# Second block of a two-block transformer kernel: gate projections moved between the query, key and value projections, head pairs every fourth chunk

## What is computed

```
h = rms_norm(x); proj = h @ w_in            # q, k, v, gate for three branches of 8 heads x 64,
                                            # q_idx (8 x 64), k_idx (64), w_idx (8), f_logit (8), merge_logit (3 x 1024)
oa = causal_attention(rope(qa), rope(ka), va) * silu(ga)
ob = causal_attention(rope(qb), rope(kb), vb, keys = top 64 of sum_h w_idx relu(rope(q_idx) . rope(k_idx))) * silu(gb)
oc = causal_attention(qc, kc, vc, logits += cumsum(log_sigmoid(f_logit + f_bias))) * silu(gc)
x  = x + (sum_n sigmoid(merge_n) * (o_n @ w_branch_n)) @ w_out
```

## Time and profile before

| | |
|---|---|
| runs of the kernel before | 1173.54 us median of 3 (1168.63 to 1174.01) |
| profiled execution | 1165.46 us, span 1163.5 us |
| PE, weight loads, DVE, ACT busy | 94%, 83%, 63%, 54% of the span |
| second block, first layer | from about 490 us to about 818 us |
| second block, second layer | from about 825 us to the end |
| mean granted PE clock | 0.975 |

### The profile page before, as it was taken

One profiled execution on the slowest core, in us unless ns is written; L12 is line 12 of the kernel. 1 busy time (PEld: TensorE's weight loads), 2 busy tenths in 40 slices (PEclk: granted clock), 3 DMA queues, 4 the chain that ended last, 5 costly groups with the idle time before them and its releaser, 6 DMA issues.

```text
span 1163.5 us, 20592 instructions
## 1 busy us (share of the span) xinstructions
PE 1090.6 (94%) x7991; PEld 966.3 (83%) x7991; DVE 736.1 (63%) x1559; ACT 627.8 (54%) x1279; POOL 2.6 (0%) x10
## 2 busy tenths in 40 slices
PE   5889999988977999989899999999998999999997
PEld 3667777766866778988899899999987998999997
DVE  4433466657465565889746776557788556766664
ACT  3344234565337654646677764445455767754443
POOL 0000000000000000000000000000000000000000
PEclk9999999998989999989999999999999999999998
DMA  9986471111313312535454566666444544566652
GB/s 317 291 260 203 150 217 52 42 55 54 100 55 90 90 57 85 157 93 143 128 145 128 141 168 181 183 185 185 119 119 118 146 127 132 160 182 183 183 178 73
DMA packets 264872, 165.04 MB, mean 142 GB/s; under 512 B 7092, under 2 KB 262824, under 8 KB 264776
## 3 DMA queue, kind: packets, MB, share of 16 engines
q1 hardware_dynamic: 264384, 163.02, 49.1%
q0 software_dynamic: 192, 0.66, 0.2%
q10 hardware_dynamic: 200, 0.06, 0.0%
HBM read 162.66 MB, written 1.05 MB: 141 GB/s over the span
## 4 chain that ended last, share of the span: by engine, by line
PE 75%; DVE 13%; ACT 6%; issue 4%; SPq 1%; DMA 1%; DVEq 0%; ACTq 0%
PE pj L1805 20%; PE pj L1806 20%; PE pj L1807 19%; DVE w_lo L1196 2%; PE tr L2250 1%; PE ac L2087 1%; PE sc L2075 1%; PE tr L1986 1%; PE sc L1979 1%; PE ac L2193 1%; ACT w_hi L743 1%; PE pj L1892 1%; DVE terms L1297 1%; PE ac L2000 1%; PE sc L2175 1%
## 5 line engine op out<-in xcount | busy, mean ns | idle before, releaser
L1805 PE MATMUL pj<-h_hi,w_hi 128*128 128x256 f32 (+1 forms) x1472 | 459.6, 312 | 14.6 <-DVE w_lo L1196 6.3
L1806 PE MATMUL pj<-h_lo,w_hi 128*128 128x256 f32 (+1 forms) x1472 | 446.7, 303 | 0.0
L1807 PE MATMUL pj<-h_hi,w_lo 128*128 128x256 f32 (+1 forms) x1472 | 446.7, 303 | 0.0
L1196 DVE TENSOR_TENSOR w_lo<-raw,w_hi 128x1024 fp32r<-128x1024 f32 (+1 forms) x258 | 309.7, 1202 | 187.9 <-ACT w_hi L743 186.9
L1805 PEld LDWEIGHTS pj<-h_hi,w_hi 128*128 128x128 f32 x1472 | 285.7, 194 | 42.9 <-issue 21.5
L743 ACT ACTIVATE w_hi<-raw 128x1024 fp32r<-128x1024 f32 (+1 forms) x258 | 267.4, 1038 | 53.9 <-PE pj L1807 53.9
L1806 PEld LDWEIGHTS pj<-h_lo,w_hi 128*128 128x128 f32 x1472 | 285.9, 194 | 10.3 <-issue 1.5
L1807 PEld LDWEIGHTS pj<-h_hi,w_lo 128*128 128x128 f32 x1472 | 285.3, 194 | 10.4
L1805 PE MATMUL pj<-m_hi,w_hi 128*128 128x256 f32 (+1 forms) x352 | 110.0, 312 | 10.1 <-DVE w_lo L1196 6.0
L1806 PE MATMUL pj<-m_lo,w_hi 128*128 128x256 f32 (+1 forms) x352 | 108.7, 309 | 0.0
L1807 PE MATMUL pj<-m_hi,w_lo 128*128 128x256 f32 (+1 forms) x352 | 108.5, 308 | 0.0
(11 more groups left out here) (308 smaller groups left out, 1319.7 us busy)
## 6 DMA issues: line engine op xcount, KB each, us to landing
raw<-in_w_in_dram SPq DMA_DIRECT2D x152, 512.0 KB, 3.8
ada_raw<-in_ada_w_dram SPq DMA_DIRECT2D x48, 512.0 KB, 6.9
raw<-in_even_w_in_dram SPq DMA_DIRECT2D x28, 512.0 KB, 4.8
raw<-in_w_branch_dram SPq DMA_DIRECT2D x24, 512.0 KB, 3.4
raw<-in_w_out_dram SPq DMA_DIRECT2D x16, 512.0 KB, 4.1
raw<-in_odd_w_in_dram SPq DMA_DIRECT2D x11, 512.0 KB, 4.1
raw<-in_even_w_out_dram SPq DMA_DIRECT2D x8, 512.0 KB, 3.7
raw<-in_odd_w_out_dram SPq DMA_DIRECT2D x8, 512.0 KB, 3.7
```

The source lines that it names most:

```text
L1196: last = nc.vector.tensor_tensor(lo, src, hi.bitcast(F32), ALU.subtract)
L1805: nc.tensor.matmul(dst, lh, rh, start=first, stop=False)
L1806: nc.tensor.matmul(dst, lh, rl, start=False, stop=False)
L1807: return nc.tensor.matmul(dst, ll, rh, start=False, stop=final)
```

## The change

Two gate chunks follow each two head pairs, from the second group on; the last two stand behind the first six `merge` chunks. Pairs move from slots 11 + 3t to 9 + 4t. The index scores move from slots 5, 7, 9, 10 to 11, 15, 19, 23, each between two pairs, the rotations of `qi_h` from slots 3, 4 to 7, 15, the rounds of the selection from slots 12 to 19 to 25 to 32, the small columns from 3 to 6, and the cumulative sum from 8 to 10. On DVE, in a pair's slot, `split_lo` and both reciprocals come straight behind `head_scores`; in other slots `split_lo` comes straight behind the evacuation. On ACT `split_hi` comes ahead of the small columns. Waits are added where `tanh` and `sc` are now shared in another order. No arithmetic and no load is added or removed; the loads come in the new order of chunks.

```diff
--- before.py
+++ after.py
@@ block2_chunks
-    out += [("g", t) for t in range(NTRIP)]
+        if t:
+            out += [("g", t - 2), ("g", t - 1)]
     for mp in range(4):
         out += [("merge", (b, 2 * mp + e)) for b in range(3) for e in range(2)]
+        if mp == 0:
+            out += [("g", NTRIP - 2), ("g", NTRIP - 1)]
         out += [("branch", (b, mp)) for b in range(3)]
@@ slots
-IDX_SLOT = {5: 0, 7: 1, 9: 2, 10: 3}
-PAIR_SLOT = {11 + 3 * t: t for t in range(NTRIP)}
-TOPK_SLOT = 12
-DECAY_SLOT = 8
-FEW_SLOT = 3
+PAIR_SLOT = {9 + 4 * t: t for t in range(NTRIP)}
+IDX_SLOT = {11 + 4 * m: m for m in range(4)}
+QI_SLOT = {7: 0, 15: 1}
+TOPK_SLOT = 25
+DECAY_SLOT = 10
+FEW_SLOT = 6
@@
+ROPE_ORDER = sorted([(2, "ki")] + [(s, ("qi", i)) for s, i in QI_SLOT.items()]
+                    + [(s + 1, c) for s, c in enumerate(B2_CHUNKS) if c[0] == "k" and BRANCH_ORDER[c[1] // 4] != FORGET])
+ROPE_ORDER = [name for _, name in ROPE_ORDER]
+
 def rope_number(pair):
-    return 3 + sum(BRANCH_ORDER[p // 4] != FORGET for p in range(pair))
+    return ROPE_ORDER.index(("k", pair))
+
+def rope_free(pair):
+    turned = [p for p in range(pair) if BRANCH_ORDER[p // 4] != FORGET]
+    return rope_number(turned[-1]) + 1 if turned else 0
@@ scalar engine
-                                h_rope_input(rope_number(i), kind == "k", scale, src)
+                                h_rope_input(rope_free(i), kind == "k", scale, src)
...
                             if i >= 2:
                                 act.wait_ge(*freed_at(G2_OF[("g", i - 2)], lay))
+                            if i < 4:
+                                act.wait_ge(is_acc, lay * 16 + (8 if i < 2 else 16))
                             nc.scalar.activation(tanh[:, i % 2, 0:SEQ], src, ACT.Tanh, scale=0.5).then_inc(tanh_set, 1)
...
+                    if 1 <= s < B2_IN:
+                        split_hi(pos(s, lay) + AHEAD)
                     if s == FEW_SLOT + 1:
                         act.wait_ge(fx_set, lay + 1)
...
-                    if 1 <= s < B2_IN:
-                        split_hi(pos(s, lay) + AHEAD)
...
                         act.wait_ge(is_done, lay * (HEADS // 2) + m + 1)
+                        if m == 2:
+                            act.wait_ge(*freed_at(G2_OF[("g", 1)], lay))
@@ vector engine
-                    if s in (3, 4):
-                        i = 2 * (s - 3)
+                    if s in QI_SLOT:
+                        i = 2 * QI_SLOT[s]
...
                         head_scores(2 * t)
                         head_scores(2 * t + 1)
+                        split_lo(pos(s, lay) + AHEAD)
+                        head_reciprocal(2 * t)
+                        head_reciprocal(2 * t + 1)
                     if 1 <= s <= B2_IN:
                         h_evacuate(s - 1)
+                    if 5 <= s < B2_IN and t is None:
+                        split_lo(pos(s, lay) + AHEAD)
...
-                    if s == FEW_SLOT + 1:
+                    if s == FEW_SLOT + 2:
...
-                    if 5 <= s < B2_IN:
-                        split_lo(pos(s, lay) + AHEAD)
-                    if t is not None:
-                        head_reciprocal(2 * t)
-                        head_reciprocal(2 * t + 1)
@@ tensor engine, index_scores and pair_scores
-                    pe.wait_ge(rope_out, ROPES1 + lay * ROPES2 + 2 + m // 2)
-                    if m >= 1:
-                        pe.wait_ge(is_relu, lay * HEADS + 2 * m)
+                    pe.wait_ge(rope_out, ROPES1 + lay * ROPES2 + ROPE_ORDER.index(("qi", m // 2)) + 1)
+                    pe.wait_ge(neg_set, lay * 48 + 4 * (m + 1))
...
                     if pair >= 1:
                         pe.wait_ge(neg_set, lay * 48 + 4 * pair)
-                    else:
-                        pe.wait_ge(is_relu, lay * HEADS + HEADS)
+                        pe.wait_ge(is_relu, lay * HEADS + 2 * min(pair, HEADS // 2))
```

More of the change, by code:

```diff
@@ L1084, in h_rope_input @@
                 def h_rope_input(n, place, scale, src):
-                    act.wait_ge(rope_out, ROPES1 + lay * ROPES2 + (n if n > 3 else 0))
+                    act.wait_ge(rope_out, ROPES1 + lay * ROPES2 + n)
                     nc.scalar.activation(rope[:, int(place), :], src, ACT.Copy, scale=scale).then_inc(freed["act"], 1)
```

## The result

The changed kernel takes 1154.15 us (median of 4 runs, 1151.86 to 1155.83) against 1173.72 (4 runs, 1168.63 to 1174.01) for the kernel before, measured beside it: 0.9842 of it, with a 95% interval of 0.9809 to 0.9875. It is faster by 19.6 us; 23.0 were forecast, with 1150.5 us and a range of 1141 to 1164.

The account below looks back on a forecast made before the run. PE, busy 94%, bounds the kernel, so only its lost time can be won. 27.8 us to be had less 2.7 for early slots and 2.2 for breaks gives 22.9, from 1173.54 to about 1150.5 us; range 1141 to 1164.

Parts of the forecast that it names:

- What was there to be had: PE's waits in both layers: 18.6 us idle, 7.4 of clock, 1.8 of tails behind eleven waits; together 27.8 us.
- Early slots: Slots 5 to 8: DVE late, so pair 0's transposes wait 1.5 us in the first layer, 1.2 in the second; cost 2.7.
- Too short for the clock: At pair 0's early wait: the granted clock would not fall, judged by a 0.6 us wait that kept 1.00.
- Breaks: PE's projection runs: seven more cuts a layer, 36 for 29, at 0.16 us each; cost 2.2 us, bounds 0 and 3.
- Pairs and rounds: Later transposes do not wait; in slots 25 to 32 DVE needs 29.2 us against PE's 28.5; cost 0.
- Gates, added waits, table loads: Gate chunks among exponentials, new waits on PE and ACT, and ACT's table loads each cost 0.
- The rounds did not collide: Rival: DVE enters slot 25 late, pair 5's probabilities come late; price 11.4 us, time 1162; chance 0.15.
- The early slots did slip further: Rival: early wait costs 7.4 us instead of 2.7; gain 18.2, time 1155.5, or 1159 with both chunks late; chance 0.15.
- Nothing was won back by late banks: Rival: DVE's waiting behind exponentials returns as late banks or w_lo, as large as the old waits; 1173 us; chance 0.06.
- no pair carried lateness on: Slower rival: DVE, held at reciprocals, carries lateness between pairs, 3.1 us a pair; 1200 us with 16 pairs; chance 0.06.

Follow-up runs that it names:

- e9: Changed kernel with gates last again, pairs in slots 11 + 3t, index scores in 13 to 22, rounds in 24 to 31, early reciprocals kept: 1143.70 us, 0.9757.
- e3: Changed kernel with the cumulative sum behind chunk 12 instead of 10: 1153.02 us, 0.9837 of the kernel before.
- e4: Changed kernel with the cumulative sum behind chunk 12 and the first rotation of qi_h in slot 10 instead of 7: 1150.43 us, 0.9813.
- e1: Changed kernel with DVE's old order inside a slot, w_lo and the reciprocals last: 1158.61 us, 0.9886 of the kernel before.
- e5: Changed kernel with a pair's values behind chunk s+3 instead of s+2, next to the next pair's scores: 1151.97 us, 0.9839.
- e2: Kernel before with only the early w_lo and reciprocals on DVE, slots and chunks untouched: 1159.10 us, 0.9889.

## Why the prediction was right, and where it was not

**Direction, range and mechanism** came as forecast. What was there to be had was put at 27.8 us. e9, which has no waits, has exactly 27.8 less in its layers. It has four cuts a layer fewer than the kernel before (1.4 us), but its index scores behind transposes cost 1.4 again, as shown below, so the waits themselves were 27.8. That the first term fits to a tenth is luck: against the second profile of the kernel before it would be 28.8, and its parts are less firm than their sum, for there were fifteen waits and not eleven, and the clock fell five times in one execution and behind two waits in the other.

**Early slots: the term that was mis-sized.** "I take 1.5 us in the first layer and 1.2 in the second" stands against idle times of 0.62 + 0.65 + 1.77 and 0.62 + 0.23 + 1.78, with 0.16 behind each of six and 1.7 of clock: 8.3 for 2.7. Two steps failed in it. The prediction counted the lateness of DVE, which was there (0.62 and 0.65), and left out the bank: the cumulative sum and the transposes take turns in two banks, and it had been moved into the very slot in which both are wanted. And "Too short for the clock" was wrong in one layer of two, for the wait there was 1.78 us. e3 and e4 take each part away.

**Breaks: counted short.** A cut costs 0.18, as priced within 0.02, and 14 of them make 2.5. Besides, "at 11 + 4m they come right behind transposes, so they cut no run" was right in words and saved nothing. From the first transpose to the index scores behind it PE takes 0.75 us, where from the first transpose to a projection it takes 0.57:

```profile
548.41 0.82 PE L2267 MATMUL tr<-const,expd 128*128 128x128 f32 x6
549.16 0.49 PE L2173 MATMUL sc<-x_t 64*128 64x128 f32 x4
```

The 0.18 is as much as a cut costs; eight times, 1.4. e9 has the same 0.75 (535.58 to 536.33). Why it is so was not tried. So 3.9 in place of 2.2.

27.8 - 8.3 - 3.9 is 15.6, and the layers gave 15.9; with the second profiles it is 28.8 - 8.3 - 3.9 = 16.6 against 16.7.

**Pairs and rounds** held: no transpose waits from pair 1 on. But the reason given was more than was needed. The prediction let the fourth chunk and the missing rotations carry the pairs along with the early reciprocals; e9 has neither and waits nowhere, and e1 shows that they carry the pairs nearly as well when the reciprocals are late (0.57 us at most). In slots 25 to 32 PE took 29.3 us, from 587.40 to 616.70, and DVE was busy for 24.7 of them, so that was less close than 29.2 against 28.5.

**Gates, added waits, table loads** cost nothing, as taken. The load before pair 0's exponentials ends 3.5 us before they can start. That the Trainium skill (ScalarE: Activation LUTs, What ACT_TABLE_LOAD costs) adds a drain of 1.38 us to it is not seen here either: the logarithm starts 1.29 us after its load begins, as in the earlier trace rows.

**The rivals.** The rounds did not collide. The early slots did slip further, and that rival's gain of 18.2 us is nearer to the layers' 15.9 than the forecast; it was priced by lateness alone. (Its time follows from its gain as 1155.3 us, not 1155.5.) Nothing was won back by late banks, and no pair carried lateness on: PE has 111.0 of 111 us busy from 534 to 645.

**Time against layers.** The medians differ by 19.6 us, the layers by 15.9 and 16.7 in two pairs of profiles. The other 3 us are not explained: the changed kernel's second execution was 3.3 us above its median while that of the kernel before was at its own, the part ahead of the layers varies by 7 us from one execution to the next, and whether it favours one kernel was not tried. That the medians lie nearer to the forecast than the layers do is luck. So the forecast of 23.0 was 6 to 7 us too high for its own mechanism and looks closer than it was.

## What to carry to other kernels

Put what the next engine waits for (here two reciprocals of 0.1 us, and `w_lo`) ahead of the work on its queue that has time (here a rotation or a round). That edit of a few lines gave by itself 11.4 us in the layers where the whole change gave 15.9, and with the index scores and rounds moved as well, and the gates left where they were, 27.8. When work is moved into a slot, check the shared banks for what else is wanted there, and not only the load of the engines. And test whether the most elaborate part of a change is the part that pays: here, with the reciprocals early, the gates between the pairs cost 2 us a layer in cuts.

## What the runs showed of the hardware

The clock's answer to a wait of about 2 us is not settled by its length. Behind the same wait of 1.77 to 1.78 us it stayed at 1.00 in four layers (both of e5, and the first layer of the changed kernel in both its profiles) and fell in two, the second layer of the changed kernel in its two profiles (0.52 in the one shown above). The kernel before fell to 0.52, 0.50 and 0.51 behind waits of 1.63, 1.99 and 2.15 in one execution, and stayed at 1.00 behind waits of 1.63, 2.54 and 2.15 in the other. In e2 it fell behind 2.24 in the first layer and stayed up behind 2.22 in the second. Behind the waits of 3.97 to 4.50 it fell every time, six of six; behind waits of 1.44 us or less in the layers of all these profiles it never did. A fall behind one of the shorter waits cost about 1.7 us.

An unchanged program ran its first 490 us in times that differ by 7 us between executions, with the granted clock at 0.97 or 0.90 in one stretch of 50 us and at 1.00 or 0.93 in another.
